# Second attention of a macaron trunk: a head's output turned behind the next head's projection 4, and output products in the last head's projection places

## The reference, cut to the mixer

```python
proj = h @ w_in
fq, fk, fv, ff, mq, mk, mv, mo, mi, mf = jnp.split(proj, ...)
y_a = forgetting_attention(fq, fk, fv, log_f_a)          # 8 heads of 64
qk = silu(causal_depthwise_conv(concat([mq, mk]), w_conv, b_conv))
h_b = mlstm_chunkwise(mq_c, mk_c, mv, i_pre, log_f_b)    # 4 heads of 128
h_b = rms_normalize(h_b) * g_mhn
y_b = sigmoid(mo) * h_b
y = concat([y_a, y_b]) @ w_out
x = x + gt2 * y
```

## Time and profile before

| | |
|---|---|
| median of three runs | 2067.47 us (2065.39 to 2070.42) |
| profiled execution: time, span of the core | 2065.87 us, 2064.1 us |
| mean granted TensorE clock | 0.965 |
| busy: TensorE, VectorE, ScalarE, GpSimd | 93%, 57%, 37%, 43% |
| TensorE, head 0's projection 4 to head 1's | 1117.71 to 1168.82 us |
| last head's projection 4 to the output stage | 1269.24 to 1315.95 us |

### The profile page before, as it was taken

How to read it: one execution, slowest core, us unless ns; L and a number is a source line. 1 busy time by engine, 2 the same in 40 slices (tenths; PEclk the granted TensorE clock), 3 DMA queues, 4 the chain that set the end, 5 groups by cost and what they waited for, 6 DMA issues and landing times. The chain is left out here.

```text
span 2064.1 us, 25546 instructions
## 1 busy us (share of the span) xinstructions
PE 1918.3 (93%) x9280; PEld 1569.7 (76%) x9280; DVE 1183.3 (57%) x1682; ACT 762.3 (37%) x1387; POOL 891.0 (43%) x636
## 2 busy tenths in 40 slices
PE   4699999999999969999998998899999999999997
PEld 3488888888888848777777776687788888888886
DVE  5966667655777751444414555448543443548777
ACT  5533233222444431544423444335232333334444
POOL 4887687674000241000012111368977877820002
PEclk7799999999999979999999999899999999999999
DMA  7256565633966201111101111132322323149662
GB/s 291 64 161 200 181 209 172 202 113 123 380 217 193 73 21 38 28 39 42 62 21 41 42 42 38 54 133 77 123 102 95 115 102 110 65 174 361 204 194 82
DMA packets 204616, 257.15 MB, mean 125 GB/s; under 512 B 14014, under 2 KB 124882, under 8 KB 202962
## 3 DMA queue, kind: packets, MB, share of 16 engines
q1 hardware_dynamic: 204498, 255.59, 37.0%
HBM read 206.71 MB, written 48.84 MB: 124 GB/s over the span
## 5 line engine op out<-in xcount | busy, mean ns | idle before, releaser
L420 POOL TENSOR_TENSOR ffn_ring_b<-ffn_raw_in,ffn_ring_b 128x512 fp32r<-128x512 f32 x174 | 247.0, 1426 | 145.1 <-ACT ffn_ring_b L415 145.1
L832 PE MATMUL bank<-ffn_w_hi,ffn_a_hi 128*128 128x512 f32 x616 | 240.1, 390 | 1.2 <-DVE ffn_w_lo L816 1.2
L834 PE MATMUL bank<-ffn_w_hi,ffn_a_lo 128*128 128x512 f32 x616 | 239.7, 389 | 0.0
L833 PE MATMUL bank<-ffn_w_lo,ffn_a_hi 128*128 128x512 f32 x616 | 239.6, 389 | 0.0
L1532 POOL TENSOR_TENSOR mx_w_lo<-mx_raw_w,mx_w_hi 128x1024 fp32r<-128x1024 f32 x29 | 73.0, 2526 | 359.6 <-ACT mx_w_hi L1363 359.5
L415 ACT CAST ffn_ring_b<-ffn_raw_in 128x512 fp32r<-128x512 f32 x174 | 107.9, 621 | 299.7 <-PE bank L1267 284.1
L108 POOL TENSOR_SCALAR rms<-rms 128x1 f32<-128x1 f32 x24 | 15.1, 628 | 444.3 <-ACT ffn_junk L102 430.5
L805 ACT CAST ffn_a_hi<-ffn_a_stage 128x512 fp32r<-128x512 f32 x154 | 95.6, 621 | 202.8 <-PE bank L834 198.5
L1086 DVE TENSOR_TENSOR ffn_u<-bank,ffn_u 128x512 f32<-128x512 f32 x111 | 76.4, 688 | 163.1 <-PE bank L1267 163.0
L1265 PE MATMUL bank<-h_hi,ffn_ring_a_hi 128*128 128x512 f32 x356 | 142.5, 400 | 26.5 <-ACT ffn_g L1014 18.2
L816 DVE TENSOR_TENSOR ffn_a_lo<-ffn_a_stage,ffn_a_hi 128x512 fp32r<-128x512 f32 x154 | 106.4, 691 | 74.6 <-ACT ffn_a_hi L805 74.6
(11 more groups left out here) (316 smaller groups left out, 4697.7 us busy)
## 6 DMA issues: line engine op xcount, KB each, us to landing
ffn_raw_in<-in_w_ffn_in SPq DMA_DIRECT2D x88, 512.0 KB, 6.0
ffn_a_stage<-hidden SPq DMA_DIRECT2D x154, 256.0 KB, 3.2
ffn_w_stage<-in_w_ffn_out SPq DMA_DIRECT2D x132, 256.0 KB, 3.2
ada_rest<-in_w_ada SPq DMA_DIRECT2D x64, 448.0 KB, 4.0
hidden<-ffn_u SPq DMA_DIRECT2D x88, 256.0 KB, 2.0
hidden<-ffn_g SPq DMA_DIRECT2D x66, 256.0 KB, 2.0
mx_raw_w<-in_w_mix_in SPq DMA_DIRECT2D x28, 512.0 KB, 3.7
ada_ring<-in_w_ada SPq DMA_DIRECT2D x8, 1024.0 KB, 12.0
```

The source lines that it names most:

```text
L420: pool.tensor_tensor(self.lo(q), self.source(b, m), self.hi(q).bitcast(F32), ALU.subtract)\
L832: pe.matmul(dst, a_hi, w_hi, start=first, stop=False, skip_group_check=True)
L833: pe.matmul(dst, a_hi, w_lo, start=False, stop=False, skip_group_check=True)
L834: mm = pe.matmul(dst, a_lo, w_hi, start=False, stop=True, skip_group_check=True)
```

## The change

The turn of head h's output is taken from the end of head h and put behind projection 4 of head h + 1; only the last head still turns its own at its end. In the last head, places 1, 2 and 3 of the missing projections get output products for the first four token tiles: k = 0 and 1 in place 1, k = 2 in place 2, k = 3 in place 3. The output stage leaves these out. ScalarE's and GpSimd's lists for the last head are set for it: the first output weight is cast behind the sigmoid, ahead of the `h_hi` copies; the second one and `h_hi` of k = 2 and 3 behind the `dec` copies; all four `y` low halves are GpSimd's (VectorE made two), in an order with the weights. The first half of the gate row has a buffer of its own, `gate_0`, so that the first two output weights can be loaded and gated before the sigmoid is done.

```diff
--- before.py
+++ after.py
@@ -1458,9 +1458,9 @@
     num_ready, inter_kept, o_done = s("num_ready"), s("inter_kept"), s("o_done")
     sq_done, var_done, rpow_done = s("sq_done"), s("var_done"), s("rpow_done")
     yb_done, ybt_ready, ybt_kept = s("yb_done"), s("ybt_ready"), s("ybt_kept")
-    gate_loaded, gated = s("gate_loaded"), s("gated_pool")
-
-    y_hi, y_lo_pool, y_lo = s("y_hi"), s("y_lo_pool"), s("y_lo")
+    gate_loaded, gate_row_loaded, gated = s("gate_loaded"), s("gate_row_loaded"), s("gated_pool")
+
+    y_hi, y_lo_pool = s("y_hi"), s("y_lo_pool")
 
     fox = ExitStack()
     fsb = lambda n, *a: core.sb(f"mx_{n}", *a, ctx=fox)
@@ -1514,6 +1514,7 @@
 
     late.close()
     gate = mo
+    gate_0 = core.at("mx_gate_0", [P, BANK], 204.375)
     states = mkT[:, :].rearrange("p (c v) -> p c v", v=V1)
     o_all = kw[:, :].rearrange("p (c v) -> p c v", v=V1)
     kw_c = kw[:, 0:S]
@@ -1647,10 +1648,12 @@
             for c, col in ((0, COL_MK), (1, COL_MQ), (2, COL_MO)):
                 ml_w(0, c, col)
             repeat(sp, MH, ml_loads)
-            sp.wait_ge(sig_done, MH)
-            sp.dma_start(gate[:, :], core.mod(gate_row)).then_inc(gate_loaded, 16)
+            sp.dma_start(gate_0[:, :], core.mod(gate_row)[:, 0:BANK]).then_inc(gate_loaded, 16)
             for n in range(2):
                 w_load(sp, n, C_O[n], w_out[:, 2 * n:2 * n + 2, 0:BANK])
+            sp.wait_ge(sig_done, MH)
+            sp.dma_start(gate[:, :], core.mod(gate_row)).then_inc(gate_row_loaded, 16)
+            sp.wait_ge(gate_row_loaded, 16)
 
         @block.gpsimd
         def _(pool):
@@ -1690,13 +1693,17 @@
                     w_cut_lo(pool, 1, h * 2 + (C_M[1] + 2))
                 else:
 
+                    pool.wait_ge(gate_loaded, 16)
+                    gate_out(ms, pool, gate_0, 0, C_O).then_inc(gated, 1)
+                    w_cut_lo(pool, 0, C_O[0])
                     for k in range(2):
                         pool.wait_ge(y_hi, k + 1)
                         cut_y_lo(pool, k, y_lo_pool)
-                    pool.wait_ge(gate_loaded, 16)
-                    for n in range(2):
-                        gate_out(ms, pool, gate, n, C_O).then_inc(gated, 1)
-                    w_cut_lo(pool, 0, C_O[0])
+                    gate_out(ms, pool, gate_0, 1, C_O).then_inc(gated, 1)
+                    w_cut_lo(pool, 1, C_O[1])
+                    for k in range(2, PAIRS):
+                        pool.wait_ge(y_hi, k + 1)
+                        cut_y_lo(pool, k, y_lo_pool)
 
                 pool.wait_ge(var_done, h + 1)
                 pool.tensor_tensor(tiny[:, 5, :], tiny[:, 4, :], core.neg_half[:, :], ALU.pow)\
@@ -1822,6 +1829,7 @@
                 act.wait_ge(x_kept, h * X_PER + X_PER)
                 act.activation(sg[:, :], mo[:, :], ACT.Sigmoid).then_inc(sig_done, 1)
                 if last:
+                    w_cut_hi(act, 0, C_O[0], freed=(x_ready, h * X_PER + 4), is_gated=(gated, 1))
                     act.wait_ge(x_ready, MH * X_PER)
                     for k in range(2):
                         act.copy(core.h_hi[:, k, :], yT_fox[:, k, :]).then_inc(y_hi, 1)
@@ -1838,7 +1846,9 @@
                 if not last:
                     keep_x(h + 1, 2, False)
                 if last:
-                    w_cut_hi(act, 0, C_O[0], freed=(x_ready, MH * X_PER), is_gated=(gated, 1))
+                    w_cut_hi(act, 1, C_O[1], freed=(x_ready, MH * X_PER), is_gated=(gated, 2))
+                    for k in range(2, PAIRS):
+                        act.copy(core.h_hi[:, k, :], yT_fox[:, k, :]).then_inc(y_hi, 1)
                 for j in range(NS):
                     r, jj = j // 3, j % 3
                     act.wait_ge(num_ready, h * 3 + (r + 1))
@@ -1849,10 +1859,6 @@
                     link(act.activation(sq_junk[:, :], o_all[:, j, 0:P], ACT.Square,
                                         accum_out=tiny[:, 0, j:j + 1]))
                 act.activation(sq_junk[:, 0:NS], tiny[:, 0, :], ACT.Copy).then_inc(sq_done, 1)
-                if last:
-                    w_cut_hi(act, 1, C_O[1], freed=(x_ready, MH * X_PER), is_gated=(gated, 2))
-                    for k in range(2, PAIRS):
-                        act.copy(core.h_hi[:, k, :], yT_fox[:, k, :]).then_inc(y_hi, 1)
                 if not last:
                     keep_x(h + 1, 3, False)
                     w_cut_hi(act, 1, h * 2 + (C_M[1] + 3), freed=(x_ready, h * X_PER + (X_PER + 4)))
@@ -1986,11 +1992,6 @@
                     .then_inc(v_kept_odd, 1)
 
             chunks = lambda t: t.rearrange("p (c s) -> p c s", s=P)
-
-            def cut_y(ks):
-                for k in ks:
-                    dve.wait_ge(y_hi, k + 1)
-                    cut_y_lo(dve, k, y_lo)
 
             def ml_body(h, first, last):
                 link.at(h)
@@ -2077,8 +2078,6 @@
                     dve.tensor_tensor(o_all[:, c4, 0:P], o_all[:, c4, 0:P],
                                       tiny[:, 6, c4].unsqueeze(2).to_broadcast([P, 4, P]), ALU.mult)\
                         .then_inc(yb_done, 1)
-                if last:
-                    cut_y(range(2, PAIRS))
                 for half in range(2):
                     dve.wait_ge(ybt_ready, h * 2 + (half + 1))
                     cols = slice(half * BANK, (half + 1) * BANK)
@@ -2245,9 +2244,29 @@
             for g in range(4):
                 project(0, g)
 
+            def turn_out(done):
+
+                for j in range(NS):
+                    if j % 4 == 0:
+                        pe.wait_ge(yb_done, done + (j // 4 + 1))
+                    mm = pe.transpose(core.bank[:, (7, 4)[j // 4], j % 4 * P:(j % 4 + 1) * P], o_all[:, j, 0:P],
+                                      core.ident[:, :])
+                    if j % 4 == 3:
+                        mm.then_inc(ybt_ready, 1)
+
+            def out_fox(k):
+
+                if k % 2 == 0:
+                    pe.wait_ge(w_lo_done[k // 2], C_O[k // 2] + 1)
+                pe.wait_ge(y_lo_pool, k + 1)
+                for t in range(NS // 2):
+                    token_product(pe, k, t)
+
             def ml_body(h, first, last):
                 c_of = lambda j: slice(j * P, (j + 1) * P)
                 project(h, 4)
+                if not first:
+                    turn_out(h * 2 - 2)
                 project(h, 5)
                 if not last:
                     project(h + 1, 0)
@@ -2265,6 +2284,10 @@
                         mm.then_inc(qk_ready, 1)
                 if not last:
                     project(h + 1, 1)
+                else:
+                    pe.wait_ge(x_kept, MH * X_PER)
+                    out_fox(0)
+                    out_fox(1)
                 for j in range(NS - 1):
                     if j in (0, 3):
                         pe.wait_ge(kw_done, h * 2 + 2)
@@ -2284,6 +2307,8 @@
                         mm.then_inc(spt_ready, 1)
                 if not last:
                     project(h + 1, 2)
+                else:
+                    out_fox(2)
                 pe.wait_ge(state_done, h * NS + NS)
                 for r in range(3):
                     num_b, int_b = ((5, 6), (7, 4), (5, 6))[r]
@@ -2302,20 +2327,8 @@
                 if not last:
                     project(h + 1, 3)
                 else:
-
-                    pe.wait_ge(x_kept, MH * X_PER)
-                    pe.wait_ge(w_lo_done[0], C_O[0] + 1)
-                    for k in range(2):
-                        pe.wait_ge(y_lo_pool, k + 1)
-                        for t in range(NS // 2):
-                            token_product(pe, k, t)
-                for j in range(NS):
-                    if j % 4 == 0:
-                        pe.wait_ge(yb_done, h * 2 + (j // 4 + 1))
-                    mm = pe.transpose(core.bank[:, (7, 4)[j // 4], c_of(j % 4)], o_all[:, j, 0:P],
-                                      core.ident[:, :])
-                    if j % 4 == 3:
-                        mm.then_inc(ybt_ready, 1)
+                    out_fox(3)
+                    turn_out(h * 2)
 
             repeat(pe, MH, ml_body)
     ms.close()
@@ -2370,7 +2383,7 @@
 
     def gpsimd(self, pool):
         ms, norm, weights, NS = self.ms, self.norm, self.weights, self.c.NS
-        for n in range(1, 8):
+        for n in range(2, 8):
             slot, c = self.at(n)
             hi, lo = self.out_w(n) if n >= 4 else (ms.w_hi[:, slot, :], ms.w_lo[:, slot, :])
             pool.wait_ge(ms.w_hi_done[slot], c + 1)
@@ -2458,7 +2471,7 @@
             if k % 2 == 0:
                 pe.wait_ge(ms.w_lo_done[slot], self.C_O[slot] + k // 4 + 1)
             for t in range(NS):
-                if k < 2 and t < NS // 2:
+                if k < KD // 2 and t < NS // 2:
                     continue
                 if t == 0 and k >= KD // 2:
                     pe.wait_ge(self.y_lo, k - KD // 2 + 1)
```

## The result

| | before | after |
|---|---|---|
| median of the comparison | 2066.43 us (2065.33 to 2070.42, 4 runs) | 2089.1 us (2088.32 to 2090.86, 4 runs) |
| ratio, 95% interval | | 1.0105, [1.0093, 1.0117] |
| profiled execution: time, span | 2065.87, 2064.1 us | 2090.86, 2089.1 us |
| last head's convolution (C), from head 0's projection 4 | 152.6 us | 165.1 us |
| C to the output stage | 45.6 us | 59.2 us |

The forecast was 2090.0 us. Before and after are the two kernels; C is the start of the last head's convolution on VectorE; a boundary is the stretch between two heads, and the turn the eight transposes of a head's output. The first finished row is taken at GpSimd's first step of the norm behind the output stage (L108).

The account below looks back on a forecast made before the run. TensorE is busy for 93% of the span, so elsewhere only its stalls can be shortened. Terms 14.7 + 13.6 - 5.45 = 22.9 us on the median of 2067.47 make 2090 us; range 2076 to 2099, the forecast case's own 2083 to 2098.

Parts of the forecast that it names:

- Projection 4 starts at the low half of `mo`: At the boundaries: projection 4 waits for GpSimd's low half of those weights, starting at 1167.7 instead of 1168.82, 1.1 us earlier.
- Term one: At the boundaries: with the turn behind projection 4, the last head's convolution starts 14.7 us later.
- clock holds: Rival, mainly at the boundaries: TensorE stays at 2.4 GHz after 4.5 us of idling, giving back 13.3 us, 2077 us; 6%.
- Term two: Last head, convolution to output stage: output products waiting for their inputs hold up `u` and `num`, 13.6 us longer.
- Term three: Output stage: 24 matmuls fewer, -5.45 us.
- GpSimd and VectorE block each other: Rival, last head: GpSimd's cuts and VectorE's passes hold each other up, total 2094 to 2096 us; 8%.
- The change does what it says: Rival, boundaries: projection 4 doesn't wait for the low half and runs from 1163.1 at full clock, total 2070 us; 3%.
- low halves in time: Rival, last head: `y` low halves and weights are ready by C + 14.5, products fill old waits, +3.4, 2071 us; 5%.

Follow-up runs that it names:

- e9: The changed kernel with 18 extra matmuls that nobody reads behind projection 3 at the three boundaries: 2082.8 us, ratio 1.0078.
- e3: The changed kernel with output products k = 0 and 1 moved from ahead of `u` to behind the `dec` transposes, with k = 2: 2080.72 us, ratio 1.0058.
- e4: The changed kernel with output product k = 2 moved behind `num`, ahead of k = 3: 2076.16 us, ratio 1.0042.
- e11: The changed kernel with VectorE's `yT_ml` product behind the convolutions, output products behind `num`, ScalarE's casts earlier, 18 unread matmuls behind projection 3: 2065.85 us.
- e12: e11 with GpSimd's row of cuts in the last head waiting for VectorE's last argument step: 2061.72 us, ratio 0.9976.
- e10: e8 with 9 and 8 unread matmuls ahead of the turn's two halves at the three boundaries: 2059.02 us, ratio 0.9962.
- e2: The changed kernel with the turn back at the end of each head: 2075.04 us, ratio 1.0032.
- e8: The changed kernel with the turn at its old place, all four output products behind `num`, ScalarE's second cast and late copies behind its exponentials: 2061.79 us.

## Why the prediction was right, point by point

**Projection 4 starts at the low half of `mo`.** Right: three starts, each behind 4.4 us of idling for L1533. From head 0's projection 4 to head 1's pass 50.13 us; 49.99 was forecast.

**Term one, 14.7 us late; measured 12.4.** The mechanism holds, and its size was off by 2.3. The forecast took 10.1 us from projection 4 to the convolution at each boundary, with 2.65 of it for the low clock. Measured are 8.98, 10.16 and 9.11. At the second boundary TensorE ran the whole window at 0.50, and projection 4 to turn took 8.2, which is 5.45 + 2.75. At the first and third it rose sooner, 0.68 in the mean of the first one's window, and took 7.15, which is 5.45 + 1.7. The same idling of 4.4 us led to two lengths of the low clock. So the mis-sized term is the 2.65 us, too high by 0.95 at two of three boundaries: 1.9 of the 2.3 us. The forecast took it from the first boundary alone. The second and third boundary before, each behind two waits of 2.1 us as well, had already shown less:

```profile
1219.80:1225.10 5.30, 5.30 (x21) 4.35 (x20) 4.32 (x5) 0.00 (x0) 1.39 (x1) 0.80 0.35 96
1269.20:1274.50 5.30, 5.30 (x17) 4.28 (x16) 4.66 (x5) 0.00 (x0) 0.00 (x0) 0.63 0.01 3
```

That the clock fell at all was the step on which the "clock holds" rival hung; e9 holds it and prices the three boundaries at 5.6 us, where that rival had 8.0. The wait for the Silu was 1.27 and 1.37 us instead of 1.8, also at the boundary with the long low clock: turn to convolution took 1.84 and 1.95 (2.0 forecast), convolution to TensorE's start behind the Silu 11.4 (11.5). The boundaries lie 52.4 and 53.5 us apart (53.6).

**Term two, 13.6 us; measured 13.6.** Of its steps, from C: `out_fox(0)` at 20.8 (19.5 forecast), `u` at 28.3 (27.5), the `dec` transposes at 30.6 (29.5), `out_fox(2)` at 38.6 (37.7), `num` at 43.0 (43.1), output stage at 59.2 (59.2). Errors of 1 us and more cancel. GpSimd's first three steps took 8.5 us instead of 7.4; VectorE's passes over `dec` and `sg` ran beside them. Against that, `out_fox(2)` took 4.45 instead of 5.35 and `out_fox(0)` and `(1)` together 7.55 instead of 8.0, the low clock being shorter here too. The waits for `h_lo` are 5.3 and 6.9 (near 7 was said for the second). e3 and e4 confirm which products carry it.

**Term three, -5.45 us; measured -5.4.** GpSimd's timeline in the output stage, before and after:

```profile
1364.04 0.19 POOL L108 TENSOR_SCALAR rms<-rms 128x1 f32<-128x1 f32 x1 [7.94 <-ACT out_junk L102]
```

```profile
1378.45 2.40 POOL L2390 TENSOR_TENSOR out_w_lo<-mx_raw_w,out_w_hi 128x1024 fp32r<-128x1024 f32 x1 [2.26 <-ACT out_w_hi L1363]
1388.67 0.19 POOL L108 TENSOR_SCALAR rms<-rms 128x1 f32<-128x1 f32 x1 [7.82 <-ACT out_junk L102]
```

1364.04 less 1315.95 is 48.1, and 1388.67 less 1345.98 is 42.7. The size hides two small errors. The forecast left the last weight's low half just hidden; in after it ended at 1380.85, behind TensorE's first half (1380.42), and TensorE, which waits for it there, stood idle for 0.5 us:

```profile
1380.95 0.47 PE L2463 MATMUL bank<-out_w_hi,h_hi 128*128 128x512 f32 x1 [0.53 <-issue]
```

Against that, the first 6 us of the stage ran at a granted clock of 0.73 instead of 0.59.

**Sum.** 12.4 + 13.6 - 5.4 = 20.6 in the trace, 22.9 forecast, 22.7 between the medians. The two microseconds between trace and medians are of the size of the unchanged part's wandering (below), so that the median hits the forecast to 1 us is partly luck: the terms are off by 2.3.

**The rivals.** "GpSimd and VectorE block each other" did happen in after, at 1302.32 to 1307.4, but cost TensorE 1.3 us at most: C to `kw` took 20.7 us (20.9 in the last head before), and TensorE was then busy with the late products until 1315.05, so that `kw` wasn't waited for. Its price of 4 to 6 us was that of one place. In e11 a row that met the four steps made C to `kw` 6.4 us longer than in e12. The Trainium skill, "SBUF — State Buffer", section "SBUF: two separate sides", says that whichever holds the shared port pair blocks the other for its whole instruction. e11 and e12 agree for the steps with two SBUF inputs, e10 (2.83 us) and e12 for the one over `sg`; the reduction at 1280.82, with one input, and the cut that began inside it kept their 1.22 and 2.35 us both. "The change does what it says" fell with the first row of the timeline, "low halves in time" with the 5.33 us at 1307.50.

## What to carry to other kernels

Work moved into a wait is worth what it overlaps only if its own inputs are ready there: put a filler product behind the work that others wait for, not ahead of it (the same 48 products lost 7.3 us in the empty places (e2), and gained 4.1 at the end (e8)). Moving a wait by a whole stage moves its consumers too, so look at who reads the moved result, and in which order that engine takes it. And beside a row of GpSimd steps each of three tiny VectorE steps took as long as the GpSimd step beside it had left (e11): let the row start behind the chain. A forecast of the low clock's price should look at every boundary of the trace, not at the first.

## What the runs showed that was not expected

- Steps over 8 numbers took 1.79 and 2.26 us instead of 0.17 (e11), back at 0.17 once GpSimd waited (e12).
- 17 or 18 extra matmuls a boundary, of 0.23 us each and read by nobody, made two kernels faster: e9 6 us below after, and e10 3.5 below e8 in the trace. In both the granted clock was 1.00 at the boundaries where it had been 0.50 to 0.79.
- Head 0's projection 4 started between 1115.65 and 1121.81 us in 14 profiled executions with the same code ahead of it, without a link to the change. Kernel before:

```profile
1117.71 0.79 PE L1541 MATMUL bank<-h_hi,mx_w_hi 128*128 128x512 f32 x1 [4.98 <-POOL mx_w_lo L1532]
```

What sets it was not tried. What lies behind the first finished row took 700.0 to 700.9 us in all 14, so the profiled spans differ by this start and by the stretch that the changes touch. A start that wanders over 6 us makes a single span worth less than a difference from a fixed point of the trace.
